# The products of the SSD mixer inside a chunk, issued in halves of 64 queries on the two column halves of TensorE's array

## What is computed

```python
L = SSD_CHUNK            # 128 tokens in a chunk; 256 tokens are 2 chunks
# 8 heads of 64 features, in 2 groups of 4 heads
cb = jnp.einsum('bclgn,bcsgn->bclsg', cm, bm)
y_diag = jnp.einsum('bclsgr,bcsgrp->bclgrp', cb[..., None] * decay, xdt)
states = jnp.einsum('bclgn,bclgrp->bcgrpn', bm, xdt * decay_to_end[..., None])
y_off = jnp.einsum('bclgn,bcgrpn->bclgrp', cm, prev) * jnp.exp(cum)[..., None]
y = y_diag + y_off + d_skip.astype(jnp.float32).reshape(G, R)[:, :, None] * xh
```

## Time and profile before

| | |
|---|---|
| median of 3 runs | 1800.2 us (1798.85 to 1801.1) |
| the profiled execution's own time | 1803.26 us |
| its span in the profile | 1801.2 us |
| PE busy | 1724.3 us, 96% of the span |
| PEld busy | 1533.2 us, 85% |
| DVE busy | 1206.7 us, 67% |
| ACT busy | 900.5 us, 50% |

### The profile page before, as it was taken

How to read it: one execution, slowest core, us unless ns; L and a number is a source line. 1 busy time by engine, 2 the same in 40 slices (tenths; PEclk the granted TensorE clock), 3 DMA queues, 4 the chain that set the end, 5 groups by cost and what they waited for, 6 DMA issues and landing times.

```text
span 1801.2 us, 36219 instructions
## 1 busy us (share of the span) xinstructions
PE 1724.3 (96%) x15070; PEld 1533.2 (85%) x15070; DVE 1206.7 (67%) x1673; ACT 900.5 (50%) x1096; POOL 44.5 (2%) x47
## 2 busy tenths in 40 slices
PE   6999999998999999999999999899999989999998
PEld 5877799987987789988888798788988877899896
DVE  5888765547678765546556767577686786487874
ACT  5564533335475343335635545355464554356772
POOL 2000000000000000000000000000000000000130
PEclk9999999998999999999999999999999999999999
DMA  8557478553548566655222322222222122352112
GB/s 197 184 190 301 141 184 195 189 192 123 179 151 309 174 169 187 188 190 164 75 83 60 87 69 62 70 72 84 60 72 79 64 95 94 99 176 71 48 56 109
DMA packets 254739, 238.35 MB, mean 132 GB/s; under 512 B 32288, under 2 KB 217680, under 8 KB 254320
## 3 DMA queue, kind: packets, MB, share of 16 engines
q1 hardware_dynamic: 253440, 233.21, 42.1%
q0 software_dynamic: 1136, 2.81, 0.6%
HBM read 234.94 MB, written 1.05 MB: 131 GB/s over the span
## 4 chain that ended last, share of the span: by engine, by line
PE 76%; DVE 10%; ACT 4%; DVEq 3%; DMA 3%; issue 2%; ACTq 1%; SPq 0%
PE pg L2547 35%; PE pg L1253 30%; PE pm L1253 6%; PE pm L2547 2%; PE pm L1256 2%; DVE ring_r L784 1%; DVEq L1741 1%; DMA ring<-in_ada_w 1%; PE pm L2550 1%; DVE ring_r L567 1%; DVE ring L1739 1%; DMA ring<-in_hg_w_in 1%; DVE ring_r L1705 1%; DVE work L1761 1%; DVE work L1739 1%
## 5 line engine op out<-in xcount | busy, mean ns | idle before, releaser
L1253 PE MATMUL pg<-ring_r,work_r 128*128 128x256 f32 (+3 forms) x1792 | 381.3, 324 | 10.6 <-DVEq L785 6.2
L567 DVE TENSOR_TENSOR ring_r<-ring,ring_r 128x2048 fp32r<-128x2048 f32 (+1 forms) x126 | 283.6, 2260 | 153.6 <-ACT ring_r L560 148.0
L2547 PE MATMUL pg<-ring_r,work_r 128*128 128x512 f32 (+1 forms) x1776 | 379.5, 374 | 5.3 <-DVEq L3019 2.9
L2547 PEld LDWEIGHTS pg<-ring_r,work_r 128*128 128x128 f32 x1776 | 308.3, 190 | 68.4 <-issue 8.4
L1253 PE MATMUL pg<-ring_r 128*128 128x256 f32 (+3 forms) x1008 | 330.7, 328 | 10.8 <-issue 5.2
L1253 PEld LDWEIGHTS pg<-ring_r,work_r 128*128 128x128 f32 x1792 | 301.4, 191 | 36.4 <-issue 6.4
L2547 PE MATMUL pg<-work_r,ring_r 128*128 128x256 f32 x2688 | 318.8, 281 | 5.9 <-DVEq L3009 3.1
L2547 PEld LDWEIGHTS pg<-work_r,ring_r 128*128 128x128 f32 x2688 | 317.4, 189 | 7.3 <-DVE ring_r L567 3.6
L560 ACT ACTIVATE ring_r<-ring 128x2048 fp32r<-128x2048 f32 (+1 forms) x126 | 237.1, 1890 | 168.5 <-DMA ring<-in_w_ffn_up 68.9
L1253 PE MATMUL pg<-work_r,ring_r 128*128 128x512 f32 (+1 forms) x976 | 265.9, 362 | 0.0
L1253 PEld LDWEIGHTS pg<-ring_r 128*128 128x128 f32 x1008 | 192.6, 191 | 27.4 <-issue 6.4
(11 more groups left out here) (380 smaller groups left out, 1854.5 us busy)
## 6 DMA issues: line engine op xcount, KB each, us to landing
ring<-in_hg_w_in SPq DMA_DIRECT2D x80, 512.0 KB, 4.0
ring<-in_w_in SPq DMA_DIRECT2D x36, 1024.0 KB, 5.2
ring<-in_ada_w SPq DMA_DIRECT2D x24, 1024.0 KB, 7.0
ring<-in_w_ffn_gate SPq DMA_DIRECT2D x44, 512.0 KB, 4.0
ring<-in_w_ffn_up SPq DMA_DIRECT2D x44, 512.0 KB, 5.3
ring<-in_w_ffn_down SPq DMA_DIRECT2D x22, 1024.0 KB, 5.0
ring<-in_w_out SPq DMA_DIRECT2D x12, 1024.0 KB, 5.0
ring<-in_ple_w_gate SPq DMA_DIRECT2D x8, 1024.0 KB, 5.2
```

The lines of the kernel that those rows point to most:

```text
L567: W.low_done(V.tensor_tensor(lo, W.raw(i, name)[:, 0:lo.shape[1]], W.hi(i, name).bitcast(f32), ALU.subtract))
L1253: return T.matmul(out_, lhsT, rhs, start=first, stop=last)
L2547: return T.matmul(out_, lhsT, rhs, start=first, stop=last)
```

## The change

Each product of `ydiag` is issued as two: the first with the 64 left columns of the stationary slice (queries 0 to 63), written to PSUM partitions 0 to 63, the second with the 64 right columns (queries 64 to 127), written to partitions 64 to 127. The moving operand, `xdt`, is the same 128 x 64 for both. The values and where they stand in PSUM are as before. The only other code that has anything to do with them, ACT's copy, is unchanged.

```diff
                 for t in range(NT):
                     for hd in range(SSD_H):
-                        last = mm(GEMM.buf("ydiag")[:, t * 512 + hd * 64:t * 512 + (hd + 1) * 64], big[:, t * 1024 + hd * P:t * 1024 + (hd + 1) * P],
-                                  xdt[:, t * 512 + hd * 64:t * 512 + (hd + 1) * 64])
+                        for q in (0, 64):
+                            at = t * 1024 + hd * P + q
+                            last = mm(GEMM.buf("ydiag")[q:q + 64, t * 512 + hd * 64:t * 512 + (hd + 1) * 64], big[:, at:at + 64],
+                                      xdt[:, t * 512 + hd * 64:t * 512 + (hd + 1) * 64])
                 GEMM.done(last)
```

## The result

| | before | changed |
|---|---|---|
| median of 20 runs | 1801.05 us (1796.52 to 1802.63) | 1804.14 us (1801.42 to 1806.23) |
| span of the profiled execution | 1801.2 us | 1803.3 us |

The changed kernel is slower: the ratio is 1.0019, with a 95% interval of 1.0012 to 1.0026, so +3.4 us (2.2 to 4.7). The median lies outside the range given, 1798.4 to 1803.2. The 20 runs of the kernel before have a median 0.85 us above the three runs that the forecast started from; less that, the changed kernel is at 1803.3, still just outside.

A forecast was written before the change was run, and what follows sets the result against it. The prediction took the DMA load `ada11` to bound both layers around `ydiag`, so PE's saving became idle time: 1800.2 - 0 = 1800.2 us against the median of the runs, range 1798.4 to 1803.2.

The forecast's parts named there:

- `ydiag` on PE: In each layer, `ydiag` on PE takes 2.0 us (1.0 to 7.5) in place of 3.52.
- the quarters: Products on array quarters, 0.0136 us a record, from which two halves were put at 0.027 us a record.
- Where PE's 1.5 us go: Behind `ydiag`: DVE takes 0.2 us, and the other 1.3 become PE idle time ahead of `ada11`.
- the term on the path is 0: In both layers, time saved at `ydiag` only lengthens PE's wait for `ada11`, so the kernel gains 0 us.
- for `ada11` until 167.67 as before: First layer, `modulation(2)`: PE still waits for this load until 167.67, the pause growing from 0.31 to about 1.6 us.
- The clock fall: Rival, chance 0.15: the second layer's 2.9 us pause halves PE's clock for `ada11`'s records and `yoff`, +2.1 us.
- The lateness of `ada11`: Rival, chance 0.05: the earlier `wo2` transfer delays `ada11` by 1.3 us in both layers, +2.6 us.
- both at once: The clock fall and the `wo2` delay together, making the kernel slower by more than 0.2%; chance 0.01.

The follow-up runs named there:

- every second head: Changed kernel with column halves, but heads 1, 3, 5 and 7 of `ydiag` left out: 1803.48 us, ratio 1.0016 against the kernel before.
- `wo2` held back: Changed kernel in which SP issues `wo2` only after `ada10` is used: 1804.36 us, ratio 1.0012 against the kernel before.
- changed again: The changed kernel, unaltered, profiled one more time: 1802.74 us, one execution.
- shorter filler: Changed kernel with one extra 128 x 128 by 512 product on PE ahead of the wait for `ada11`: 1803.04 us, ratio 1.0008 against the kernel before.

## Why the prediction was wrong

**`ydiag` on PE.** Right: 2.02 us for 2.0. The records have the form 128*64 that was foretold. Between 32 records (1.08 us, every second head) and 64 (2.02) one costs 0.029 us, for 0.027 worked out from the quarters. So the records take 1.88 us for 1.74 and the rest 0.14 for 0.3; that the sum fits to the hundredth is partly luck.

**Where PE's 1.5 us go.** Right down to `modulation(2)`, which began 9.51 us after `modulation(1)` (163.88 - 154.37), as forecast (163.3 - 153.79). With an on-time load the pause would have been 1.5 us; the kernel with half the products left out shows it, at a ratio of 1.0005 (0.9994 to 1.0016).

**The step that failed** is "the term on the path is 0", and in it the sentence that PE would wait "for `ada11` until 167.67 as before". It holds that `ydiag` cannot start the transfer earlier; it passed over that the edit could make it end later. Twice the products are also twice the instructions, and I counted their time on PE but not their bytes: 64 instructions are 4 KB in a layer, and they moved a 16 KB packet of the program from 13.2 and 12.9 us to 10.6 and 9.0, amid the four loads whose end is on the path. `ada11` then landed at 14.9 and 15.1 us, where 13.9 is in time, so the term was 1.0 to 1.4 us a layer and not 0, and with it came the fall of the clock. Shown by the kernel before with 64 instructions ahead, which has the late loads without the halves, and by the halves without the 64 instructions, which have a landing at 13.8 us. The page had the queue, with its 122 packets; the prediction passed over it, with its share of 0.5%. The rows of before also held the effect: the 11.40 us of the second layer, which the prediction gave to chance or `wo2`, belong to a packet at 12.9 us.

**The rivals.** The clock fall had 0.15 and one layer, at +2.1 us. It occurred in both layers of the first profile of the changed kernel and in one of the second. Its price was too high: with `ada11` at about 15 us the transposes of y come at 27.2 to 27.6 us without a fall (five layers among before, changed again, `wo2` held and the 64 instructions) and at 28.5 to 29.2 with it (five layers), 1.6 us between the means. The fall comes only after the 16 records have begun, so they and `yoff` run partly at full. DVE's work behind `yoff` takes as long as ever, and PE catches up beside it. The lateness of `ada11` had 0.05 and +2.6, by `wo2`. Its size was right, 1.0 to 1.4 us a layer, its cause was not: with `wo2` held back the load is late all the same. The prediction priced the two singly and gave both at once 0.01. They go together: a load that lands 1.2 us later is what stretches the pause of 1.5 us to 2.7, and of nine layers with pauses of 2.4 to 3.1 us in sum the clock fell in seven, in none with up to 1.8 us.

**The sum of what was measured.** Against before, with two profiles each: the two layers' transposes of y at 53.6 and 52.5 us in sum before, at 57.5 and 56.4 changed, +3.9 us, for +3.4 (2.2 to 4.7) of the runs. Of that, about 2 us are late loads (late in four layers of four, for one of four, at 1.25 us each, two layers to an execution: 2 x 0.75 x 1.25 = 1.9) and about 2 the clock (three layers of four at 1.56 us: 2.3). The shorter filler agrees: it takes the clock's part away and leaves a ratio of 1.0008, with an interval that also holds 1. Against the +3.9 stands the 1.3 us gained at the second place, which leaves +2.6, inside the interval of the runs.

How often the clock falls in an execution is read from two profiles only, so the split is an estimate. The runs bear it out in part: the mean granted clock is 0.9933 in the changed kernel (20 runs), 0.9935 with `wo2` held (11), 0.9945 with the short filler (11), and 0.9951 and 0.9955 in the kernel before (35 and 33). The fall behind `modulation(2)` lasts 3.4 us, which at half is 0.0009 of the span, so the filler is worth about one fall an execution. It stays open what the rest is. One candidate is a fall near 436 us that every profile has: the 700 records of PE around it take 109.8 to 109.9 us in six profiles and 111.5 to 112.1 in six others, and the second group has one of the two profiles of before and both of the changed kernel.

## What to carry to other kernels

Where an engine waits for a load, count for an edit not only its time but also its instructions: in these traces the program comes over the same DMA engines as the data, and a packet of it amid a load made the load late by 1.0 to 1.5 us. An edit that lengthens the program moves every later packet, for worse at one place and for better at another, so a difference of this size need not come from what was edited. Time taken from an engine ahead of such a wait was worth nothing here, and together with a late load it cost the clock, so fill the pause with work that needs nothing of the load, or take the chain that follows off the load, before making what precedes it faster. Two small rivals that feed each other have to be priced together.

## What the runs showed of the hardware

A 16 KB packet of the program took 1.1 us of one DMA engine. With one amid the loads, fifteen of a 1 MB load's sixteen parts landed as without it and the last one 1.0 to 1.5 us late, while all engines together moved some 370 GB/s. Products on the two column halves, 64 stationary and 64 moving columns of float32, came at 0.029 us a record, against 0.110 at full width. Semaphore waits that are long fulfilled cost PE about 0.11 us an instruction (28.86 us to the first transposes with 192 of them, 34.25 with 240).
